# Entering a second transformer layer in another order, and fetching and rounding its third weight unit by quarters

## What is computed

```python
def second_block(x, ...):
    for l in range(2):
        h = rmsnorm(x, g_pre_mix[l])
        y = token_mixer(h, w_in[l], ...)      # projections, window attention, mLSTM, w_out
        x = x + rmsnorm(y, g_post_mix[l])
        h = rmsnorm(x, g_pre_ffn[l])
        y = conv_ffn(h, w_up[l], ffn_conv_w[l], w_down[l])
        x = x + rmsnorm(y, g_post_ffn[l])
    return x
```

## Time and profile before

| | us |
|---|---|
| median of 3 runs | 2846.56 |
| lowest and highest | 2842.35, 2853.2 |
| span of the profiled execution | 2845.1 |

### The profile page before, as it was taken

The page is one execution under the profiler, slowest core; times in us unless marked ns, Lnnn a source line. Parts: engine busy times, 40 slices in busy tenths (PEclk is TensorE's granted clock), DMA queues, the critical chain, the costliest instruction groups (busy, mean ns, idle before and its releaser), DMA issues.

```text
span 2845.1 us, 36675 instructions
## 1 busy us (share of the span) xinstructions
PE 2645.0 (93%) x14324; PEld 1888.1 (66%) x14324; DVE 1227.8 (43%) x2422; ACT 877.2 (31%) x1666; POOL 828.8 (29%) x1146
## 2 busy tenths in 40 slices
PE   8999999999988888888888899999999999899998
PEld 8997777887533333333333377688888777788887
DVE  4333735224633333333333366553431475643422
ACT  3343334333211111111111144543332345433332
POOL 4343334553000000000000043335555233355554
PEclk9999999999999999999999999999999999999999
DMA  4222221325999999999999931022322221122322
GB/s 146 89 91 104 75 74 67 109 89 226 389 427 428 428 428 428 429 428 428 428 429 428 413 133 60 30 89 89 113 94 89 87 97 60 60 89 89 115 92 74
DMA packets 127719, 572.26 MB, mean 201 GB/s; under 512 B 10848, under 2 KB 58336, under 8 KB 102496
## 3 DMA queue, kind: packets, MB, share of 16 engines
q1 hardware_dynamic: 122336, 561.08, 49.6%
q10 hardware_dynamic: 5248, 9.32, 1.0%
HBM read 566.12 MB, written 4.26 MB: 200 GB/s over the span
## 4 chain that ended last, share of the span: by engine, by line
PE 64%; DMA 24%; DVE 7%; ACT 3%; POOL 1%; issue 1%; SPq 0%; POOLq 0%; DVEq 0%; ACTq 0%
PE ps L377 40%; DMA wide<-in_moe_w 18%; PE ps L1449 8%; DMA arena<-in_moe_w 5%; PE ps L1929 3%; PE ps L1908 2%; POOL ring_r L345 1%; PE ps L1896 1%; PE ps L1949 1%; PE ps L627 1%; PE ps L591 1%; PE ps L1915 1%; PE ps L606 1%; PE ps L2968 1%; PE ps L1229 1%
## 5 line engine op out<-in xcount | busy, mean ns | idle before, releaser
L345 POOL TENSOR_TENSOR ring_r<-ring,ring_r 128x256 fp32r<-128x256 f32 (+2 forms) x1120 | 813.9, 766 | 1932.8 <-ACT ring_r L326 1932.8
L377 PE MATMUL ps<-xnT_r,ring_r 128*128 128x512 f32 (+1 forms) x1664 | 484.9, 374 | 4.6 <-POOL ring_r L345 4.6
L377 PE MATMUL ps<-ring_r,xnT_r 128*128 128x512 f32 (+1 forms) x1360 | 443.8, 397 | 8.8 <-POOL ring_r L345 2.4
L377 PEld LDWEIGHTS ps<-xnT_r,ring_r 128*128 128x128 f32 x1664 | 304.5, 188 | 63.0 <-POOL ring_r L345 6.7
L377 PE MATMUL ps<-ring_r,arena_r 128*128 128x512 f32 x1392 | 332.2, 398 | 0.0
L377 PEld LDWEIGHTS ps<-ring_r,xnT_r 128*128 128x128 f32 x1360 | 288.5, 224 | 52.8 <-issue 7.1
L377 PE MATMUL ps<-xn_r,ring_r 128*128 128x512 f32 (+1 forms) x832 | 310.3, 373 | 0.0
L377 PEld LDWEIGHTS ps<-ring_r,arena_r 128*128 128x128 f32 x1392 | 265.8, 192 | 59.6 <-issue 2.9
L326 ACT ACTIVATE ring_r<-ring 128x1024 fp32r<-128x1024 f32 (+2 forms) x284 | 271.0, 1024 | 87.0 <-DMA ring<-in_w_down 68.4
L1929 PE MATMUL ps<-wide,arena 128*32 128x512 f32 x768 | 191.0, 642 | 92.0 <-DMA wide<-in_moe_w 92.0
L1929 PEld LDWEIGHTS ps<-wide,arena 128*32 128x32 f32 x768 | 53.0, 116 | 228.2 <-issue 228.2
(11 more groups left out here) (386 smaller groups left out, 3495.4 us busy)
## 6 DMA issues: line engine op xcount, KB each, us to landing
wide<-in_moe_w SPq DMA_DIRECT2D x143, 2048.0 KB, 32.9
arena<-in_moe_w SPq DMA_DIRECT2D x47, 2048.0 KB, 32.9
ring<-in_w_in SPq DMA_DIRECT2D x24, 2048.0 KB, 8.4
ring<-in_w_up SPq DMA_DIRECT2D x22, 2048.0 KB, 8.6
ring<-in_w_down SPq DMA_DIRECT2D x10, 2048.0 KB, 7.8
ring<-in_w_out SPq DMA_DIRECT2D x6, 2048.0 KB, 7.9
ring<-in_w_in SPq DMA_DIRECT2D x8, 512.0 KB, 8.8
ring<-in_w_ret_branch SPq DMA_DIRECT2D x2, 2048.0 KB, 8.1
```

The source lines that it names most:

```text
L345: ins = nc.gpsimd.tensor_tensor(ring_r[:, q % 2, piece], ring[:, q % 2, piece], ring_r[:, 2 + q % 2, piece].bitcast(F32), ALU.subtract)
L377: ins = nc.tensor.matmul(bank, left, right, start=(start and k == 0), stop=(stop and k == 2))
```

## The change

It has two parts.

1. *The entry of the second layer* (`l == 1`). ScalarE loads the Sqrt table first, then rounds quarters 0 to 2 of unit 0, takes root y0, rounds quarter 3, and goes on with y1 and h0; y2 comes behind the copies of turned tile 0, between h1 and y3. VectorE makes the low halves of three quarters, and POOL that of the fourth. VectorE does following 0 between the two operations L3362 and L3363 of branch 1, then the low half of turned tile 0, and branches 2 and 3 one and two places later than before (branch 3 now behind the low half of tile 1, following 2 and rope 0). The first layer's entry keeps its order.
2. *The third unit* (QK), in both layers. TensorE counts each of the first three quarters of unit 0 as it is used by the last AQ job; SyncE waits for each count and fetches that quarter of unit 2 by a transfer of its own (512 KB), the fourth when the whole unit is used. Each has its own semaphore. ScalarE rounds quarters 0 and 1 behind the third rot copy and quarters 2 and 3 behind the fourth, instead of all four behind the second AKV job.

Which instructions compute what is unchanged. The diff, less its semaphore names and repeated lines:

```diff
+        third_loaded = [stage_sems[n] for n in ("chosen", "gated", "half_gated", "rows_normed")]
+        first_quarter_used = stage_sems["x_returned"]
...
                 a.wait_ge(quarter_loaded[parts[0]], 16)
             elif parts[0]:
-                pass
+                if current["l"] is not None and q == Q_QK:
+                    a.wait_ge(third_loaded[parts[0]], 16)
...
             else:
-                if q or current["l"]:
+                if q == Q_QK:
+                    a.wait_ge(third_loaded[0], 16)
+                elif q or current["l"]:
                     wait_layer_unit(a, q)
...
-            for part in range(4):
+            for part in range(3):
                 cols = unit_quarter(0, part)
                 v.wait_ge(half_high, quarter_count(0, part))
                 nc.vector.tensor_tensor(ring_r[:, 0, cols], unit_home(0)[:, cols], ring_r[:, 2, cols].bitcast(F32),
                                         ALU.subtract).then_inc(half_low, 1)
+
+        def first_low_pool(pool):
+
+            cols = unit_quarter(0, 3)
+            pool.wait_ge(half_high, quarter_count(0, 3))
+            pool.wait_ge(half_low, quarter_count(0, 2))
+            n = (cols.stop - cols.start) // LOW_PIECES
+            for at in range(cols.start, cols.stop, n):
+                piece = slice(at, at + n)
+                ins = nc.gpsimd.tensor_tensor(ring_r[:, 0, piece], unit_home(0)[:, piece], ring_r[:, 2, piece].bitcast(F32), ALU.subtract)
+            ins.then_inc(half_low, 1)
...
+        def load_third_unit(sp, l):
+            src = layer_units(l)[Q_QK][1]
+            sp.wait_ge(stage_open, l + 1)
+            sp.sem_inc(stage_left, 1)
+            for part in range(4):
+                if part < 3:
+                    sp.wait_ge(first_quarter_used, part + 1)
+                else:
+                    sp.wait_ge(unit_used, l * LAYER_UNITS + (U_LAYERS + slot_free(Q_QK)))
+                dst = ring[:, layer_slot(Q_QK), unit_quarter(Q_QK, part)].rearrange("p (c n) -> p c n", n=BANK)
+                sp.dma_start(dst, src[:, 2 * part:2 * part + 2]).then_inc(third_loaded[part], 16)
...
-                    sp.wait_ge(unit_used, l * LAYER_UNITS + (U_LAYERS + slot_free(q)))
-                    load_unit(sp, l, q)
+                    if q == Q_QK:
+                        load_third_unit(sp, l)
+                    else:
+                        sp.wait_ge(unit_used, l * LAYER_UNITS + (U_LAYERS + slot_free(q)))
+                        load_unit(sp, l, q)
                     if q == 2:
                         sp.dma_start(rows[:, 3], layer_row("g_post_ffn_2", l).partition_broadcast(P)).then_inc(post_row_loaded, 16)
...
@@ -2596,6 +2627,8 @@
                 ins.then_inc(Z.proj_ready, 1)
                 if i == NT - 1:
                     release_unit(pe)
+            elif q == Q_AQ and i == NT - 1 and c % 2:
+                ins.then_inc(first_quarter_used, 1)
...
-                    for root in ((("h", 1), ("y", 3)), (("h", 2),), (("h", 3),), ())[k]:
+                    for root in ((("h", 1), ("y", 3)) if current["l"] == 0 else (("h", 1), ("y", 2), ("y", 3)), (("h", 2),), (("h", 3),), ())[k]:
                         enter_root_act(a, *root)
...
                                              scale=DH ** -0.5).then_inc(Z.turned_kept, 1)
+                        if k == 2:
+                            high_act(a, Q_QK, (0,))
+                            high_act(a, Q_QK, (1,))
+                        elif k == 3:
+                            high_act(a, Q_QK, (2,))
+                            high_act(a, Q_QK, (3,))
...
-                    if i == 1:
+                    if i == 1 and q + 1 != Q_QK:
                         high_act(a, q + 1)
...
+                return [("y", 0), ("y", 1), ("h", 0), ("y", 2), ("h", 1), ("y", 3), ("h", 2), ("h", 3)]
+            return [("y", 0), ("y", 1), ("h", 0), ("h", 1), ("y", 2), ("y", 3), ("h", 2), ("h", 3)]
...
             if current["l"]:
-                high_act(a, 0)
                 nc.scalar.activation(small[:, 30:31], table("eps"), ACT.Sqrt)
-            enter_root_act(a, "y", 0)
-            enter_root_act(a, "y", 1)
-            enter_root_act(a, "h", 0)
-            enter_root_act(a, "y", 2)
-            if current["l"]:
+                high_act(a, 0, (0, 1, 2))
+                enter_root_act(a, "y", 0)
+                high_act(a, 0, (3,))
+                enter_root_act(a, "y", 1)
+                enter_root_act(a, "h", 0)
                 a.wait_ge(half_low, quarter_count(0, 3))
...
-                term = Y.enter_term[:, i % 2]
-                link(nc.vector.scalar_tensor_tensor(out=term, in0=down_banks(i), scalar=rstd, in1=rows[:, 3], op0=ALU.mult, op1=ALU.mult))
-                nc.vector.tensor_tensor(h[:, i, :], h[:, i, :], term, ALU.add).then_inc(Z.tile_added, 1)
+                link(nc.vector.scalar_tensor_tensor(out=Y.enter_term[:, i % 2], in0=down_banks(i), scalar=rstd, in1=rows[:, 3], op0=ALU.mult, op1=ALU.mult))
+                if between:
+                    between()
+                nc.vector.tensor_tensor(h[:, i, :], h[:, i, :], Y.enter_term[:, i % 2], ALU.add).then_inc(Z.tile_added, 1)
...
+                v.wait_ge(pre_row_loaded, current["l"] * 16 + 32)
                 enter_branch_dve(v, link, 0)
-                enter_branch_dve(v, link, 1)
-                v.wait_ge(pre_row_loaded, current["l"] * 16 + 32)
-                following(0)
+                enter_branch_dve(v, link, 1, between=lambda: following(0))
+                x_turn_dve(v, 0, ENTER_BANKS[0], Z)
+                following(1)
                 enter_branch_dve(v, link, 2)
+                x_turn_dve(v, 1, ENTER_BANKS[1], Z)
+                following(2)
+                rope_tile_dve(v, 0)
+                enter_branch_dve(v, link, 3)
+                x_turn_dve(v, 2, ENTER_BANKS[2], Z)
+                following(3)
+                rope_tile_dve(v, 1)
...
-            x_turn_dve(v, 0, ENTER_BANKS[0], Z)
-            if not current["l"]:
+                x_turn_dve(v, 0, ENTER_BANKS[0], Z)
                 last_add_dve(v, 3)
-            following(1)
-            if not current["l"]:
+                following(1)
                 enter_branch_dve(v, link, 2)
-            enter_branch_dve(v, link, 3)
-            x_turn_dve(v, 1, ENTER_BANKS[1], Z)
-            following(2)
-            rope_tile_dve(v, 0)
-            x_turn_dve(v, 2, ENTER_BANKS[2], Z)
-            following(3)
-            rope_tile_dve(v, 1)
...
             for l in range(LAYERS):
                 current["l"] = l
+                if l:
+                    first_low_pool(pool)
                 for q in (1, 2, 3, 4, 5):
                     low_pool(pool, q)
```

More of the change, by code:

```diff
@@ L2424, in slot_free @@
             return q - 1
-        slot_units = [[q for q in range(1, LAYER_UNITS) if layer_slot(q) == k] for k in range(2)]
+        slot_units = [[q for q in range(1, LAYER_UNITS) if layer_slot(q) == k and q != Q_QK] for k in range(2)]
         def wait_layer_unit(eng, q):
@@ L3322, in enter_root_act @@
             base = BRANCH if what == "y" else NEXT
-            n = i if last else ENTER_ROOTS.index((what, i))
+            n = i if last else enter_roots().index((what, i))
             if what == "h":
@@ L3352, in last_act, with enter_branch_dve @@
                 enter_root_act(a, "y", i, last=True)
-        def enter_branch_dve(v, link, i, last=False):
-            v.wait_ge(Z.roots_ready, (i if last else ENTER_ROOTS.index(("y", i))) + 1)
+        def enter_branch_dve(v, link, i, last=False, between=None):
+            v.wait_ge(Z.roots_ready, (i if last else enter_roots().index(("y", i))) + 1)
             rstd = small[:, BRANCH + 8 + i:BRANCH + 9 + i]
```

10 lines of the change are left out of this document (8 added, 2 removed).

## The result

The changed kernel takes 2829.40 us (median of 4 runs, 2829.0 to 2831.47) against 2844.45 for the kernel before (median of 4, 2840.35 to 2853.2): a ratio of 0.9945, interval 0.9926 to 0.9964. That is 15.0 us faster, 0.53% by the two medians and 0.55% by the ratio. The profiled span fell from 2845.1 to 2827.3 us, by 17.8, where the sum said 13.2.

What follows compares the result with a forecast made beforehand. TensorE, busy 93% of the 2845.1 us span, was taken as the bound. Entry 6.0 plus third unit 7.2 made 13.2 us, so span 2831.9 and, with medians 1.5 above it, 2833.4 us; range 2829 to 2841.

Steps and rivals of the forecast that it cites:

- the sum: Both parts together: 6.0 us from layer 1's entry plus 7.2 from the third unit, 13.2 us in all.
- 7.0 won by tile 1's turn: Layer 1's entry: tile 1's transposes at 2246.4 instead of 2253.45, from less idle time and products at full clock.
- new wait ahead of job 2: Layer 1's entry: tile 3's branch stands behind two turns, so TensorE waits 0.9 to 1.0 us; bounds 0 and 1.8.
- its hold of 0.3: Layer 1's entry: POOL's pieces hold VectorE's L3363, taken as 0.3 us, between 0 and 0.7.
- The third unit: Behind the AKV jobs: waits for POOL's low halves go, 4.2 us in layer 1 and 3.0 in layer 0.
- The transfer of 512 KB: Third unit's fetch: a lone quarter takes 4 us from issue to rounding, bounds 0 and 9.2.
- The clock didn't fall at the entry: Rival at layer 1's entry: POOL's holds delay the first transposes and the clock falls; costs 4 us, 2837.5; chance 0.13.
- VectorE wasn't held in the AKV jobs: Rival in the AKV jobs: POOL's 11 us beside them hold VectorE, costing 9 us, 2842.5; chance 0.07.
- the rounding wasn't bound by something else: Rival at the third unit: rounding still bound by something behind AKV, only the entry counts, 2840.6; chance 0.05.
- no job ran slow: Rival at the entry's first four jobs: clock stays low, 4.6 us more per job; four give 2851.8; chance 0.03.
- How the numbers follow: Closing step on the total: 14.2 us is the 0.5% bound; within 0.66, faster 0.32, slower 0.02.
- a larger gain: Rival on the total: over 16 us, from no new wait at job 2 or a faster later stretch; 2829; chance 0.05.

Runs made afterwards that it cites:

- low4_vector: The changed kernel with all four low quarters of the second layer's unit 0 on VectorE, none on POOL; 2832.62 us, one run.
- turn_after_add: The changed kernel with following 0 (tile 0's L3370) put back behind both operations of branch 1, not between them; 2828.16 us, one run.
- third_only: The kernel before with only the third unit by quarters, in both layers, and the second layer's entry as before; 2835.10 us (9 runs), ratio 0.9963.
- changed_again: The changed kernel itself, run once more in 5 rounds; 2831.01 us against 2847.32 for the kernel before, ratio 0.9945.

## Why the prediction was right and where it was wrong

**The entry: the mechanism right, the sum right partly by luck.** The forecast was 7.0 won by tile 1's turn, less 1.0 for a new wait ahead of job 2, so 6.0; measured, 6.6 less 0.5, so 6.2 by tile 3's turn. Two errors of 0.4 to 0.5 us cancel. The table load, the early root and POOL's quarter went as worked out: the square of root 0 starts 7.7 us ahead of the last down product's end, where the step had 7.6. Tile 0's transposes start 0.43 us behind that end, where the step, its hold of 0.3 included, had them 0.2 behind (2240.9 against 2240.69). That 0.2 is the hold: it was 0.52 (1.75 - 1.23, the second being low4_vector's row for the same operation without POOL), within the bounds of 0 to 0.7. Another 0.2 is the way from the transposes to the first product, 2.2 us (2233.48 to 2235.66) where the step had 2.0. Together they are the 0.4 missing from the 7.0. The Trainium skill, "SBUF — State Buffer", section "Who interferes with whom", has such pairs exclude each other for whole instructions; the 0.52 is in line with it, and so are POOL's four pieces, 3.82 us here against the 2.8 of a quarter of a unit.

The new wait at job 2 is there, at half its forecast size. From tile 2's turn to tile 3's is 7.34 us (2245.56 to 2252.90), against 6.86 in the kernel before (2259.84 to 2266.70): 0.5 lost, of which the record shows 0.23 as idle. VectorE was as late as the step said; what the step left out is the rot of tile 0, four transposes that TensorE has to do there in both kernels ahead of job 2's products. In the kernel before the first product behind them starts at 2263.16, 0.36 us after this row:

```profile
2262.80 0.60 PE L2568 MATMUL ps<-cst,arena 128*128 128x128 f32 x4
```

In the kernel after it is 0.83 us from their start to that product (2248.52 to 2249.35).

**The third unit: right.** Forecast 4.2 and 3.0 us; measured 4.3 and 3.1 by the rows at the quarters, 4.1 and 3.1 by the stretches. The transfer of 512 KB, put at 4 us between 0 and 9.2, takes 3.7. Only the weight of the reasons was off: the step gave both the early fetch and the early rounding as what makes room, and each alone gives all but 0.3 to 0.6 us a layer. The gate chain shortened threefold (516 to 175 ns) and TensorE waited for nothing new behind it.

**The rivals.** The clock didn't fall at the entry (0.43 and 1.03 idle), VectorE wasn't held in the AKV jobs (no waits of turns or products for it there), the rounding wasn't bound by something else, and no job ran slow. turn_after_add shows in its one trace that the first of these rivals was real: 1 us more idle, and the clock was low in the windows from 2234 to 2240, at a price of 1.5 us, not 4.

**The step that failed is "How the numbers follow", with the baseline and the tail that it took.** The sum put the changed pieces at 13.2 and they are 13.4. But 14.2 us was the bound of 0.5%, and the sum lay 1 us inside it. "Within" got 0.66 and "faster" 0.32, with only 0.05 for "a larger gain" over 16 us and no term for stretches that the change doesn't touch. Nor is 0.5% what a measurement can tell from no change, as that step had it: the interval of four runs beside four is 0.9926 to 0.9964, some 5 us to either side, and third_only's 0.37% was clear of no change too. A gain of 13.2 us would have been told from none. Two things then carried the time over:

1. The gain by medians is 15.0 us here and 16.3 in changed_again, 1.8 to 3.1 over the sum. The unchanged stretches hold 4.2 us of the profiled difference, and changed_again shows that such stretches move by up to 2.8 us between executions of one program. That these stretches ran partly at the lower level could be read in the trace of before, and the prediction had no line for it; with a scatter of both signs around 13.2 and the bound at 14.2, "faster" deserved nearly one half. The clock of the kernel before in two of them (decays and later turns of layer 1's mLSTM; columns as in the clock views above):

```profile
2392.00:2407.00 15.00, 13.88 (x52) 0.89 0.37 141
...
2437.00:2452.00 15.00, 13.69 (x52) 0.77 0.37 116
```

2. The baseline. The sum was taken from 2846.56, a median of 3 runs; the one with the fourth run is 2844.45, 2.1 lower. All 31 runs of the kernel before in this study have a median of 2845.3, and all 9 of the changed kernel 2830.55. Their difference is 14.8 us, 0.52%, and resampling these runs gives 13.0 to 16.5 us for the difference of the means.

So of the 4.0 us between 2833.4 and 2829.4, 2.1 are the baseline and 1.9 the gain. With intervals of 0.9926 to 0.9964 and 0.9931 to 0.9959 the ratio includes 13.2 us (0.9954) as well as 15: the runs don't show that the mean gain is more than the two parts. That stays open. What they do show is that the two parts have their cause in the change; for the 1.6 us beyond them (14.8 less 13.2) no cause in the change was found, and none was ruled out.

## What to carry to other kernels

Cut both traces at the same instructions before explaining a difference: what changed in stretches without a changed instruction may be clock and scatter alone, and a second profile of the same kernel tells its size. When a forecast lies near the bound of what can be measured, count such stretches as a term of their own, and take the baseline from many runs. For a unit that is wanted soon behind its slot's last use, fetch it in pieces; the first piece's arrival, not the last one's, then sets when the engines behind it can start. And when you forecast a wait, list all that the waiting engine still has to do before it: even four short transposes cut a forecast wait in half here.

## What the runs showed of the hardware

- TensorE's clock after idle time isn't set by the idle time alone. 1.74 and 1.03 us of idle around eight transposes kept it at 1.00 (low4_vector), 1.38 and 1.03 around the same transposes lost it (turn_after_add: 0.50, then 1.00 again from 2240). These are one trace each. One stretch of one program had 0.79 and 0.52 in one execution and 1.00 throughout in another.
- Eighteen transposes of a constant in idle time ahead of an entry kept the clock there and shortened the stretch from the first to the fourth turn by 1.8 to 2.0 us. In both traces with this filler it took 19.5 us, in the eleven of the other kernels 21.2 to 22.4.
- VectorE and POOL, both on SBUF operands: a 1024-column sum took 1.75 against 1.23 us, POOL's four pieces of 256 columns 3.82 us against 2.8, and the chain of 16-column operations 516 against 175 ns each (the first of each pair beside the other engine's work).
- A transfer of 512 KB could be used 3.7 us after its issue, with three more behind it.
